# A hybrid decoder step on one core: three halves of the output projection take six mixed tiles first, and the samples' head norm takes one root per partition

## The chip, the cores and the metric

The kernel runs on one core of one Trainium2 chip. The metric is device time in microseconds (us) of one execution, as the median of several runs. Lower is better. Engines are named as in the profile: PE is TensorE's matmul, PEld its weight load, DVE is VectorE, ACT is ScalarE, POOL is GpSimd, and SP is the engine that issues most of the loads.

## The reference

One layer of a decoder, for a prompt of 512 tokens and for 8 samples of one token each (so 520 token columns), with model width 1024:

```python
xn = rmsnorm(x, ln1_w);  z = xn @ w_in                       # q, k, v of group A; q, k, v of group B; out-gate, i, f
attn = moba_attention(qa, k_all, v_all, q_start)             # 8 heads x 64
h, C, n, m = mlstm_chunkwise(qm, km, vm, i_pre, f_pre, ...)  # 4 heads x 128
h = h * lax.rsqrt(jnp.mean(h * h, axis=-1, keepdims=True) + RMS_EPS)
h = h * mlstm_norm_w.reshape(M_HEADS, M_HEAD_DIM)
h = (h.reshape(B, S, MLSTM_WIDTH) * jax.nn.sigmoid(om)).astype(x.dtype)
mix = jnp.concatenate([attn, h], axis=-1)
x = x + mix @ w_out
x = x + jnp.square(jax.nn.relu(rmsnorm(x, ln2_w) @ w_up)) @ w_down
```

A final RMSNorm follows. Outputs are y for prompt and samples, the keys and values of group A, and the new mLSTM states C, n and m. For the samples, the old states C and n are inputs.

## The kernel before

Activations lie transposed: 128 features of one tile on the partitions, the 520 token columns along the free side. Each factor of a product is split in a high and a low fp32r part, and a product is three matmuls (high x high, high x low, low x high), written out in `three` at L869 to L871.

The kernel works through a list of halves, `HALVES`. A half is one tile of 128 output features (`g`) for one part of the tokens: half 0 is the prompt's first 256 tokens, half 1 the other 256 and the 8 samples (264 columns). Entries 0 to 55 are the input projection (g 0 to 27), from 56 on comes the output projection (g 28 to 35). Its first three tiles run half 0 for all three (entries 56, 57, 58) and then half 1 for all three (59, 60, 61), since `LATE_X` is 3. Then both halves of each tile follow. Each half goes over eight tiles k of the inner dimension, 24 matmuls in all, into one of three accumulator banks (`acc`, entry modulo 3), and may start when the half three entries earlier is evacuated (`s_acc_evac`).

For the output projection the inner tiles are the eight mixed tiles: k 0 to 3 are attention (`att_o`), k 4 to 7 the four mLSTM heads. `mixed(k)` makes entry 56 wait for each tile in turn. The heads' tiles are made in tasks `om` and `om_mix`: DVE multiplies by the gate (L2346), ACT rounds to the high part (L1662), DVE subtracts for the low part (L2351). The last two heads are done at slot 55.

`plan()` sets for each entry (slot) the tasks that follow it, and each engine walks the same list in order and does its share of each task. Small results pass through four scratch banks of PSUM (`scr`), used in a ring: `open_job` makes PE wait until the job four places earlier is evacuated, `full` makes a reader wait until the job is written, `free` and `evacuated` report the reading.

The samples' mLSTM output is normalised per head in tasks `sm_den`, `sm_out` and `sm_end`. The values lie as 128 features by 32 columns (8 samples x 4 heads) in `sm_h`. At `sm_out` PE sums the squares over the partitions with a matrix of ones (L1066), with the sum in every partition, and transposes the new n state (L1069). DVE scales the sums and adds eps (L2136), and POOL takes the power -0.5 of all 128x32 values with `rsqrt` (L1814). At `sm_end` DVE waits for POOL (L2142), multiplies (L2143), applies the norm's weights (L2144) and the gate (L2147), and writes the high and low parts into the samples' columns of the mixed tiles (L2151, L2152). The last of these steps raises `s_smp_mix` to 3. PE waits for that ahead of entry 59, the first half 1 of the output projection, and SP ahead of the load of the final norm's weights, which has the last output weights queued behind it.

Weight tiles pass through four slots. ACT makes the high part (L1411) and POOL the low part (L1418) from tile 20 on. Tile 31 is split at slot 56, so in POOL's order its low part stands behind the root of slot 55. SP loads the next weights when `s_w_lo_ok` reaches a count.

From slot 60 on the residual is added and the MLP's input is made: PE transposes the tokens (`xt`, L1214), DVE adds, and tasks `x2` on ACT and DVE scale, split and form the MLP's operands.

Of the kernel before, what the change touches and what calls it, by code (L numbers as in the profile page):

```python
# [24 lines left out]
ALU = mybir.AluOpType  # L25
# [6 lines left out]
P = 128  # L32
# [62 lines left out]
def width(half):  # L95
    return TOK - SPLIT_TOK if half else SPLIT_TOK
# [42 lines left out]
def plan():  # L139
# [3 lines left out]
    def at(s, *names):  # L143
        tasks[s] += names
# [65 lines left out]
        at(51 + two, ("sm_rt", two))  # L210
    at(54, ("sm_den",))
    at(55, ("sm_out",))
    at(56, ("sm_end",))
    for s, j in ((60, 3), (61, 0), (61, 4), (62, 1), (62, 5), (63, 2), (63, 6), (64, 7)):
        if j == 0:
            at(s, ("xt_s",))
# [4 lines left out]
    for t in range(4):  # L221
# [2 lines left out]
    scratch = {  # L224
        "par2": 1, "rstd": 1, "xn": 1, "gates": 1, "gcols": 1, "qs_tok": 1, "qb": 1, "vs_tok": 1, "tokk": 1, "tokv": 1, "tokm": 2,
        "sm_prep": 2, "sm_c": 1, "sm_r": 1, "sm_rt": 1, "ml_m": 1, "ml_k": 3, "ml_o": 2, "ml_t": 1, "ml_mc": 1,
        "sm_den": 1, "sm_out": 2, "ks_tok": 1, "gate": 1, "mx_t": 1, "own": 1, "va_s": 1, "mx_b": 1,
        "zsum": 1, "att_s": 2, "att_t": 3, "att_o": 1, "pv_pick": 1, "pv_end": 1, "xt": 1, "xt_s": 1,
    }
    jobs = {}  # L230
# [132 lines left out]
def build(nc, x_prompt, x_sample, cache_k, cache_v, page_table, state_C, state_n, state_m, ln1_w, w_in,  # L363
# [4 lines left out]
    with ctx:  # L368
# [298 lines left out]
        def free(ins, *key):  # L667
            ins.then_inc(scr_free[JOBS[key] % 4], 1)
# [197 lines left out]
        def _(pe):  # L866
# [34 lines left out]
            def done(mm):  # L901
                mm.then_inc(s_scr_full, 1)
# [15 lines left out]
            def every(col, n=P):  # L918

                return col.to_broadcast([n, P])  # L920
# [30 lines left out]
            def task(name, *a):  # L951
# [111 lines left out]
                elif name == "sm_out":  # L1063
                    pe.wait_ge(s_sm_dve, 2)
                    out = open_job(pe, "sm_out", 0)
                    done(pe.matmul(out[:, 0:NS * MH], every(ones[:, :]), sm_t[:, :, :].rearrange("p a b -> p (a b)"),  # L1066
                                   start=True, stop=True))
                    out = open_job(pe, "sm_out", 1)
                    done(pe.transpose(out[0:NS * MH, 0:P], sm_n[:, :, :].rearrange("p a b -> p (a b)"), ident[:, :]))  # L1069
                elif name == "ml_m":  # L1070
                    h, = a

# [162 lines left out]
            def norm_to_rows():  # L1235

                pe.wait_ge(s_rs2_pow, 2)
                for parts, out in ((range(NT), scr[:, 3, :]), ((NT,), scr[:, 2, :])):
# [3 lines left out]
                                       ident[0:m, 0:m], start=True, stop=True)  # L1242
                    mm.then_inc(s_rows_up, 1)

            def mixed(k):
                if k < 4:
                    evacuated(pe, "att_o", k, 0)
                else:
                    pe.wait_ge(s_mix_lo, k - 3)

            for i in range(N_HALVES):
                if i == 0:
                    pe.wait_ge(s_xs_ok, 1)
                    half_gemm(i, x_parts, x_split_1)
                elif i == WSLOTS:
                    half_gemm(i, x_parts, x_split_0)
                elif i < 2 * N_IN:
                    half_gemm(i, x_parts)
                else:
                    if HALVES[i] == (G_OUT, 1):  # L1260
                        pe.wait_ge(s_smp_mix, 3)
                    half_gemm(i, mix_parts, mixed if i == 2 * N_IN else None)
                for name in TASKS[i]:
                    task(*name)

            def y_to_tok(i, part):

# [543 lines left out]
        def _(pool):  # L1811
            def rsqrt(x, n, free_size):

                return pool.tensor_tensor(x, x, power[0:n, :].to_broadcast([n, free_size]), ALU.pow)  # L1814
# [37 lines left out]
            def task(name, *a):  # L1852
                if name == "score":
                    b, c = a
                    n = 4 * b + c
                    if c == 0:
                        evacuated(pool, "qb", b, 0)
                    for j in (2 * c, 2 * c + 1):
                        pool.wait_ge(kv_in[j], 16 * (b + 1))
                    if n >= 2:  # L1860
                        pool.wait_ge(s_kred_ok, n - 1)
                    pool.tensor_tensor(prod[:, n % 2, :].rearrange("p (j n) -> p j n", j=2),  # L1862
                                       kv[:, 2 * c:2 * c + 2, :],
                                       Qb[:, b % 2:b % 2 + 1, :].to_broadcast([P, 2, AW]), ALU.mult)\
                        .then_inc(s_kmul_ok, 1)
                elif name == "gate":
                    pool.wait_ge(s_kred_ok, 4 * NS)
                    pool.memset(S_wide[:, :, :, :], 0.0).then_inc(s_pv_zero, 1)
                    pool.wait_ge(s_kmul_ok, 4 * NS)
                    pool.memset(vs_split[:, :].bitcast(F32), 0.0).then_inc(s_sel_ok, 1)  # L1870
                elif name == "s_put":
                    b, = a

                    if b >= 4:
                        page_used(pool, b - 4, PAGES - 1)
                    else:
                        pool.wait_ge(s_samp_exp, 1)
                        pool.wait_ge(s_pv_zero, 1)
                    pool.tensor_copy(S_wide[:, b % 4, :, AH * (b % 4):AH * (b % 4 + 1)], S[:, b, :, :])\
                        .then_inc(s_s_put, 1)  # L1880
                elif name == "sm_c":
                    b, = a
                    pool.wait_ge(s_sm_b_ok, 1)
                    pool.wait_ge(C_in[b], 16)
                    pool.tensor_tensor(state(b), state(b), sm_b[:, :, 0, b:b + 1].to_broadcast([P, MH, MD]), ALU.mult)\
                        .then_inc(s_C_decayed, 1)
                elif name == "sm_out":
                    evacuated(pool, "sm_out", 0)
                    rsqrt(sm_t[:, :, :].rearrange("p b h -> p (b h)"), P, NS * MH).then_inc(s_sm_pow, 1)
                elif name == "ml_m":  # L1890
                    h, = a
                    evacuated(pool, "ml_m", h, 0)
                    for j in range(NT):

                        blk = mA[:, A_COL[j]:A_COL[j] + P]
                        pool.affine_select(out=blk, in_=blk, compare_op=ALU.is_ge, fill=0.0, base=0,
                                           pattern=[[1, P]], channel_multiplier=-1).then_inc(s_ml_tri, 1)
                elif name == "ml_n":
                    h, = a
                    pool.wait_ge(s_ml_ms, h + 1)  # L1900
                    rsqrt(m_rs[:, :], P, NT).then_inc(s_ml_pow, 1)
# [54 lines left out]
        def _(dve):  # L1956
            chain = [0]

            def link(ins):

                chain[0] += 1
                ins.then_inc(s_dve_chain, 1)
                dve.wait_ge(s_dve_chain, chain[0])
# [54 lines left out]
            def task(name, *a):  # L2018
# [114 lines left out]
                    dve.tensor_tensor(sm_t[:, :, :], sm_h[:, :, :], sm_h[:, :, :], ALU.mult).then_inc(s_sm_dve, 1)  # L2133
                elif name == "sm_out":
                    out = full(dve, "sm_out", 0)
                    free(dve.tensor_scalar(sm_t[:, :, :].rearrange("p b h -> p (b h)"), out[:, 0:NS * MH],  # L2136
                                           1.0 / MD, EPS, ALU.mult, ALU.add), "sm_out", 0)
                    out = full(dve, "sm_out", 1)
                    free(dve.tensor_copy(n_new_rows[:, :], out[0:NS * MH, 0:P]), "sm_out", 1)
                elif name == "sm_end":  # L2140

                    dve.wait_ge(s_sm_pow, 1)  # L2142
                    link(dve.tensor_tensor(sm_h[:, :, :], sm_h[:, :, :], sm_t[:, :, :], ALU.mult))  # L2143
                    link(dve.tensor_tensor(sm_h[:, :, :], sm_h[:, :, :],  # L2144
                                           par[:, 16:20].unsqueeze(1).to_broadcast([P, NS, MH]), ALU.mult))
                    dve.wait_ge(s_om_sig, MH)
# [522 lines left out]
```

## Time and profile before

| | us |
|---|---|
| median of 3 runs | 751.14 |
| lowest and highest run | 748.95, 752.32 |
| the profiled execution, its own time | 749.44 |
| its span | 747.70 |
| PE busy (share of the span) | 699.8 (94%) |
| PEld busy | 650.9 (87%) |
| DVE busy | 467.4 (63%) |
| ACT busy | 301.6 (40%) |
| POOL busy | 294.8 (39%) |

A time in the trace is in us from the span's start. The span is divided as follows: the input projection, attention, the mLSTM heads and the samples' work up to about 315 us, the output projection from 314.9 to about 375, the MLP up to the end. A row of the trace gives an instruction's start, its duration, engine and line, the operation, and in brackets the idle time of the engine before it and what ended that. Matmuls are pipelined, so the distance between the starts of two is their price, not the duration of one.

### The profile page before, as it was taken

Reading aid. Unit: us, or ns where it says so; the run is one execution under the profiler, and the core shown is the slowest. Engines: PE = TensorE matmul, PEld = TensorE weight load, DVE = VectorE, ACT = ScalarE, POOL = GpSimd, SP = SyncE. Lnnn points to the kernel's source line nnn. Section 1 sums busy time; section 2 is a strip of 40 time slices with the busy share of each in tenths; the row PEclk is TensorE's granted clock in tenths of the full one; section 3 lists DMA queues with packets and bytes.
Section 4 is the critical chain, followed back from the end, with each engine's and each line's share of the span. In section 5 each row is a group of like instructions: output and inputs, shape, how many; then the busy total and the mean of one; then the engine's idle time right before and its main releaser. Section 6 shows DMA issues by size and latency. Waiting matters only on the chain.

```text
span 747.7 us, 15193 instructions
## 1 busy us (share of the span) xinstructions
PE 699.8 (94%) x5537; PEld 650.9 (87%) x5537; DVE 467.4 (63%) x932; ACT 301.6 (40%) x576; POOL 294.8 (39%) x215
## 2 busy tenths in 40 slices
PE   5999789797999999889878999999999999999997
PEld 5988678686878787689868999999999999999996
DVE  4387978766352438434987868575756757586133
ACT  5342454533445223125653544435234433534322
POOL 5225987831232335154002361706144160704531
PEclk8999999998999999989989999999999999999999
DMA  7716998742556968821112232423313141332202
GB/s 243 212 46 208 269 282 249 202 144 74 168 147 197 279 196 176 259 83 61 57 57 60 104 122 59 134 92 113 114 57 112 59 163 59 113 113 85 86 1 115
DMA packets 88634, 100.42 MB, mean 134 GB/s; under 512 B 5374, under 2 KB 64338, under 8 KB 88570
## 3 DMA queue, kind: packets, MB, share of 16 engines
q1 hardware_dynamic: 74566, 92.91, 40.1%
q10 hardware_dynamic: 14004, 6.67, 3.5%
q8 instruction: 39, 0.64, 0.4%
q14 instruction: 25, 0.20, 0.1%
HBM read 92.92 MB, written 6.64 MB: 133 GB/s over the span
## 4 chain that ended last, share of the span: by engine, by line
PE 78%; DVE 11%; ACT 4%; issue 2%; DMA 2%; POOL 1%; SPq 0%; ACTq 0%; DVEq 0%; POOLq 0%
PE acc L869 6%; PE acc L870 6%; PE acc L871 6%; PE acc L1335 5%; PE acc L1334 5%; PE acc L1336 5%; PE acc L1321 4%; PE acc L1320 4%; PE acc L1322 4%; PE scr L1335 3%; PE scr L1334 3%; PE scr L1320 3%; PE scr L1336 3%; PE scr L1322 3%; PE scr L1321 3%
## 5 line engine op out<-in xcount | busy, mean ns | idle before, releaser
L869 PE MATMUL acc<-act_hi,w_hi 128*128 128x256 f32 (+1 forms) x416 | 123.8, 298 | 1.1 <-DVE zT L2411 1.1
L870 PE MATMUL acc<-act_lo,w_hi 128*128 128x256 f32 (+1 forms) x416 | 119.0, 286 | 0.0
L871 PE MATMUL acc<-act_hi,w_lo 128*128 128x256 f32 (+1 forms) x416 | 118.9, 286 | 0.0
L1919 POOL TENSOR_TENSOR h_lo<-relu,h_hi 128x520 fp32r<-128x520 f32 x32 | 43.9, 1373 | 187.6 <-ACT h_hi L1735 187.2
L1862 POOL TENSOR_TENSOR prod<-kv,Qb 128x1024 f32<-128x1024 f32 x32 | 82.8, 2614 | 42.9 <-DVE S L2088 25.2
L869 PEld LDWEIGHTS acc<-act_hi,w_hi 128*128 128x128 f32 x416 | 80.2, 193 | 8.1 <-issue 4.8
L1418 POOL TENSOR_TENSOR w_lo<-raw,w_hi 128x1024 fp32r<-128x1024 f32 x20 | 47.5, 2378 | 96.7 <-ACT w_hi L1411 96.7
L870 PEld LDWEIGHTS acc<-act_lo,w_hi 128*128 128x128 f32 x416 | 80.3, 193 | 0.0
L871 PEld LDWEIGHTS acc<-act_hi,w_lo 128*128 128x128 f32 x416 | 80.0, 192 | 0.0
L2430 DVE TENSOR_TENSOR xT<-acc,xT 128x260 f32<-128x260 f32 x64 | 26.4, 427 | 55.1 <-PE acc L1336 55.1
L2411 DVE TENSOR_TENSOR zT<-acc,rstd 128x264 f32<-128x264 f32 (+1 forms) x56 | 23.5, 423 | 55.6 <-PE acc L871 49.6
L1334 PE MATMUL acc<-h_hi,w_hi 128*128 128x260 f32 x200 | 56.8, 284 | 0.0
L1335 PE MATMUL acc<-h_lo,w_hi 128*128 128x260 f32 x200 | 56.6, 283 | 0.0
L1336 PE MATMUL acc<-h_hi,w_lo 128*128 128x260 f32 x200 | 56.5, 282 | 0.0
L1411 ACT ACTIVATE w_hi<-raw 128x1024 fp32r<-128x1024 f32 x36 | 37.7, 1054 | 37.5 <-PE acc L871 33.4
L1726 ACT ACTIVATE w_hi<-w_sum 128x512 fp32r<-128x512 f32 x47 | 28.7, 627 | 59.6 <-DVE w_sum L2445 25.4
L1734 ACT ACTIVATE relu<-relu 128x520 f32<-128x520 f32 x32 | 20.4, 637 | 70.1 <-DVE relu L2524 70.1
L869 PE MATMUL acc<-mix,w_hi 128*128 128x264 f32 (+1 forms) x128 | 39.0, 305 | 6.2 <-DVE mix L2351 2.9
L2088 DVE TENSOR_REDUCE S<-prod 128x16 f32<-128x1024 f32 x32 | 38.3, 1210 | 8.0 <-POOL prod L1862 8.0
L1335 PE MATMUL scr<-h_lo,w_hi 128*128 128x260 f32 x144 | 40.8, 283 | 0.0
L1334 PE MATMUL scr<-h_hi,w_hi 128*128 128x260 f32 x144 | 40.6, 282 | 0.0
L1336 PE MATMUL scr<-h_hi,w_lo 128*128 128x260 f32 x144 | 40.6, 282 | 0.0
(408 smaller groups left out, 2296.3 us busy)
## 6 DMA issues: line engine op xcount, KB each, us to landing
kv<-in_cache_k_dram SPq DMA_DIRECT2D x64, 256.0 KB, 3.2
kv<-in_cache_v_dram SPq DMA_DIRECT2D x64, 256.0 KB, 3.3
raw<-in_w_up_dram SPq DMA_DIRECT2D x16, 1024.0 KB, 5.5
raw_d<-in_w_down_dram SPq DMA_DIRECT2D x12, 1024.0 KB, 5.0
raw<-in_w_in_dram SPq DMA_DIRECT2D x14, 512.0 KB, 6.0
raw<-in_w_in_dram SPq DMA_DIRECT2D x7, 1024.0 KB, 6.8
x_tok<-in_x_prompt_dram SPq DMA_DIRECT2D x8, 512.0 KB, 9.1
raw<-in_w_out_dram SPq DMA_DIRECT2D x4, 1024.0 KB, 6.4
```

The lines of the kernel that those rows point to most:

```text
L869: pe.matmul(out, w_hi[:, slot, k, :], hi[k][:, cols], start=(n == 0), stop=False)
L870: pe.matmul(out, w_hi[:, slot, k, :], lo[k][:, cols], start=False, stop=False)
L871: mm = pe.matmul(out, w_lo[:, slot, k, :], hi[k][:, cols], start=False, stop=(n == KT - 1))
L1320: pe.matmul(out, u_hi[n % RING][:, k, :], hi[k], start=(k == 0), stop=False)
L1321: pe.matmul(out, u_hi[n % RING][:, k, :], lo[k], start=False, stop=False)
L1322: mm = pe.matmul(out, u_lo[n % RING][:, k, :], hi[k], start=False, stop=(k == 3))
L1334: pe.matmul(out, w[0], h_hi[:, k, cols], start=first, stop=False)
L1335: pe.matmul(out, w[0], h_lo[:, k, cols], start=False, stop=False)
L1336: mm = pe.matmul(out, w[1], h_hi[:, k, cols], start=False, stop=last)
L1418: eng.tensor_tensor(w_lo[:, slot, :, :], raw[:, r_slot, :, side * P:(side + 1) * P], w_hi[:, slot, :, :].bitcast(F32), ALU.subtract).then_ ...
L1862: pool.tensor_tensor(prod[:, n % 2, :].rearrange("p (j n) -> p j n", j=2), kv[:, 2 * c:2 * c + 2, :], Qb[:, b % 2:b % 2 + 1, :].to_broadca ...
L1919: pool.tensor_tensor(h_lo[:, t, :], relu2[:, t % 2, :], h_hi[:, t, :].bitcast(F32), ALU.subtract).then_inc(s_hs_lo, 1)
```

## The change

Three things are edited.

A new function `first_outputs` replaces the loop for entry 56. It runs entries 56, 57 and 58 together: first k 0 to 5 of each of the three, then k 6 and 7 of each. The waits for the mixed tiles stay with entry 56's matmuls. Entries 57 and 58 are skipped in the main loop, and only their tasks are walked.

`sm_out`'s sum of squares exchanges its operands: the squares (128x32) are the weights and one column of ones moves, so 32 sums come out, one on each of 32 partitions. DVE scales them into `mx_col`, and POOL takes the root of 32x1.

A new task `sm_rs` at slot 56 copies the roots to all partitions: PE multiplies the column, broadcast to 128, by a 32x32 identity, into a scratch bank. PE does it between k 6, 7 of entry 57 and k 6, 7 of entry 58, and waits there for POOL. `sm_end`'s first multiplication reads this bank in place of `sm_t`, and a wait on its evacuation stands in place of the chain's step.

```diff
-    at(56, ("sm_end",))
+    at(56, ("sm_rs",), ("sm_end",))
...
                 elif name == "sm_out":
                     pe.wait_ge(s_sm_dve, 2)
                     out = open_job(pe, "sm_out", 0)
-                    done(pe.matmul(out[:, 0:NS * MH], every(ones[:, :]), sm_t[:, :, :].rearrange("p a b -> p (a b)"),
+                    done(pe.matmul(out[0:NS * MH, 0:1], sm_t[:, :, :].rearrange("p a b -> p (a b)"), ones[:, :],
                                    start=True, stop=True))
...
+                elif name == "sm_rs":
+                    pe.wait_ge(s_sm_pow, 1)
+                    out = open_job(pe, "sm_rs", 0)
+                    done(pe.matmul(out[:, 0:NS * MH], every(mx_col[0:NS * MH, :], NS * MH), ident[0:NS * MH, 0:NS * MH],
+                                   start=True, stop=True))
...
+            def first_outputs():
+
+                for ks in (range(6), range(6, KT)):
+                    for i in range(2 * N_IN, 2 * N_IN + LATE_X):
+                        g, half = HALVES[i]
+                        if ks[0] == 0:
+                            pe.wait_ge(s_acc_evac, i - 2)
+                            pe.wait_ge(s_w_lo_ok, g + 1)
+                        for k in ks:
+                            if i == 2 * N_IN:
+                                mixed(k)
+                            three(acc[:, i % 3, 0:width(half)], g % WSLOTS, mix_parts, token_half(half), k, k)
+                        if ks[0] and i == 2 * N_IN + 1:
+                            task("sm_rs")
...
-                else:
+                elif i == 2 * N_IN:
+                    first_outputs()
+                elif i >= 2 * N_IN + LATE_X:
                     if HALVES[i] == (G_OUT, 1):
                         pe.wait_ge(s_smp_mix, 3)
-                    half_gemm(i, mix_parts, mixed if i == 2 * N_IN else None)
+                    half_gemm(i, mix_parts)
                 for name in TASKS[i]:
-                    task(*name)
+                    if name[0] != "sm_rs":
+                        task(*name)
...
                 elif name == "sm_out":
                     evacuated(pool, "sm_out", 0)
-                    rsqrt(sm_t[:, :, :].rearrange("p b h -> p (b h)"), P, NS * MH).then_inc(s_sm_pow, 1)
+                    rsqrt(mx_col[0:NS * MH, :], NS * MH, 1).then_inc(s_sm_pow, 1)
...
                     out = full(dve, "sm_out", 0)
-                    free(dve.tensor_scalar(sm_t[:, :, :].rearrange("p b h -> p (b h)"), out[:, 0:NS * MH],
-                                           1.0 / MD, EPS, ALU.mult, ALU.add), "sm_out", 0)
+                    free(dve.tensor_scalar(mx_col[0:NS * MH, :], out[0:NS * MH, 0:1], 1.0 / MD, EPS, ALU.mult, ALU.add),
+                         "sm_out", 0)
...
                 elif name == "sm_end":
 
-                    dve.wait_ge(s_sm_pow, 1)
-                    link(dve.tensor_tensor(sm_h[:, :, :], sm_h[:, :, :], sm_t[:, :, :], ALU.mult))
+                    out = full(dve, "sm_rs", 0)[:, 0:NS * MH].rearrange("p (b h) -> p b h", b=NS)
+                    free(dve.tensor_tensor(sm_h[:, :, :], out, sm_h[:, :, :], ALU.mult), "sm_rs", 0)
+                    evacuated(dve, "sm_rs", 0)
```

## Rows read from the trace of the kernel before

**Rows 1.** The page's chain that ended last, shares of the span by engine.

```profile
PE 78%; DVE 11%; ACT 4%; issue 2%; DMA 2%; POOL 1%; SPq 0%; ACTq 0%; DVEq 0%; POOLq 0%
```

**Rows 2.** Stretches: length, busy of PE, PEld, DVE, ACT, POOL (count), PEclk, DMA.

```profile
302.10:304.10 2.00, 0.00 (x0) 0.00 (x0) 0.43 (x1) 0.00 (x0) 0.00 (x0) 1.00 0.93 245
...
317.15:319.19 2.04, 0.16 (x2) 0.00 (x1) 1.34 (x3) 1.16 (x2) 0.00 (x0) 1.00 0.00 0
319.19:321.18 1.99, 0.97 (x3) 0.67 (x4) 1.26 (x3) 1.41 (x2) 0.00 (x0) 0.52 0.00 0
321.18:326.04 4.86, 4.86 (x22) 4.86 (x23) 0.78 (x3) 0.17 (x1) 4.61 (x1) 0.50 0.03 7
```

**Rows 3.** Instructions in order of time, PE, 315 to 331: start, duration, line, tiles.

```profile
315.13 0.28 PE L870 MATMUL acc<-mix,w_hi 128*128 128x256 f32 x1
...
317.03 0.28 PE L871 MATMUL acc<-mix,w_lo 128*128 128x256 f32 x1
319.19 0.54 PE L869 MATMUL acc<-mix,w_hi 128*128 128x256 f32 x1 [1.88 <-DVE mix L2351]
...
321.18 0.58 PE L869 MATMUL acc<-mix,w_hi 128*128 128x256 f32 x1 [1.02 <-DVE mix L2351]
...
321.99 0.41 PE L869 MATMUL acc<-mix,w_hi 128*128 128x256 f32 x1
...
325.83 0.41 PE L869 MATMUL acc<-mix,w_hi 128*128 128x256 f32 x1
...
330.25 0.39 PE L869 MATMUL acc<-mix,w_hi 128*128 128x264 f32 x1 [0.57 <-DVE mix L2152]
```

**Rows 4.** Instructions in order of time, DVE, 318 to 323.

```profile
318.44 0.69 DVE L2351 TENSOR_TENSOR mix<-zT,mix 128x512 fp32r<-128x512 f32 x1 [0.70 <-ACT mix L1662]
...
320.43 0.69 DVE L2351 TENSOR_TENSOR mix<-zT,mix 128x512 fp32r<-128x512 f32 x1 [0.70 <-ACT mix L1662]
321.16 0.19 DVE L2136 TENSOR_SCALAR sm_t<-scr 128x32 f32<-128x32 f32 x1
...
322.23 0.42 DVE L2421 COPY xT<-acc 128x256 f32<-128x256 f32 x1 [0.69 <-PE acc L871]
```

**Rows 5.** Instructions in order of time, POOL and DVE, 321 to 330.

```profile
321.43 5.42 POOL L1814 TENSOR_TENSOR sm_t<-sm_t,power 128x32 f32<-128x32 f32 x1 [10.61 <-DVE sm_t L2136]
326.81 2.39 POOL L1418 TENSOR_TENSOR w_lo<-raw,w_hi 128x1024 fp32r<-128x1024 f32 x1
...
326.88 2.36 DVE L2143 TENSOR_TENSOR sm_h<-sm_h,sm_t 128x32 f32<-128x32 f32 x1 [4.23 <-POOL sm_t L1814]
329.28 0.19 DVE L2144 TENSOR_TENSOR sm_h<-sm_h,par 128x32 f32<-128x32 f32 x1
329.50 0.21 DVE L2147 TENSOR_TENSOR sm_h<-sm_h,zT 128x32 f32<-128x32 f32 x1
```

**Rows 6.** Groups by shape, POOL's other roots: count, busy us, mean ns, idle before.

```profile
L1814 POOL TENSOR_TENSOR rs<-rs,power 8x1 f32<-8x1 f32 x2 | 1.4, 717 | 0.0
...
L1814 POOL TENSOR_TENSOR rs<-rs,power 128x4 f32<-128x4 f32 x1 | 1.0, 1006 | 37.6 <-DVE rs L2558 37.6
...
L1814 POOL TENSOR_TENSOR y_ms<-y_ms,power 8x1 f32<-8x1 f32 x1 | 0.5, 542 | 0.0
```

**Rows 7.** Instructions in order of time, POOL and DVE, 308 to 311.

```profile
308.44 2.38 POOL L1418 TENSOR_TENSOR w_lo<-raw,w_hi 128x1024 fp32r<-128x1024 f32 x1 [9.48 <-ACT w_hi L1411]
...
309.98 0.42 DVE L2411 TENSOR_TENSOR zT<-acc,rstd 128x256 f32<-128x256 f32 x1 [2.61 <-PE acc L871]
```

**Rows 8.** One line's instructions, mx_b's copy: ns min/median/max, first and last start.

```profile
L1138 PE MATMUL scr<-ident,mx_col x2: 272/296/319, 183.1 to 183.2; 64*128 64x64 f32 x2
```

**Rows 9.** Instructions in order of time, SP's queue: loads issued after 330.

```profile
330.22 0.34 SPq L825 DMA_DIRECT2D lnf_b<-in_lnf_w_dram  x1
...
339.99 52.88 SPq L846 DMA_DIRECT2D raw<-in_w_up_dram  x4
```

**Rows 10.** The chain that ended last, piece by piece: start, us, what.

```profile
348.02 0.89 PE scr L1214 x8
```

More of the change, by code:

```diff
@@ L226, in plan @@
         "sm_prep": 2, "sm_c": 1, "sm_r": 1, "sm_rt": 1, "ml_m": 1, "ml_k": 3, "ml_o": 2, "ml_t": 1, "ml_mc": 1,
-        "sm_den": 1, "sm_out": 2, "ks_tok": 1, "gate": 1, "mx_t": 1, "own": 1, "va_s": 1, "mx_b": 1,
+        "sm_den": 1, "sm_out": 2, "sm_rs": 1, "ks_tok": 1, "gate": 1, "mx_t": 1, "own": 1, "va_s": 1, "mx_b": 1,
         "zsum": 1, "att_s": 2, "att_t": 3, "att_o": 1, "pv_pick": 1, "pv_end": 1, "xt": 1, "xt_s": 1,
```

## The prediction

> **What bounds the kernel now.** I read the chain that ended last first: TensorE carries 78% of it [rows 1]. So time comes off only where TensorE stands still or runs slowly on that chain. Next I read the granted clock over the start of the output projection, and there TensorE's column shows both faults. From 317.15 to 319.19 us it is busy 0.16 of 2.04 us. From 319.19 to 321.18 it is busy 0.97 of 1.99 us, now at a granted clock of 0.52. From 321.18 to 326.04 it is busy throughout, at 0.50, which is the 1.2 GHz level [rows 2]. TensorE's own instructions give the reasons [rows 3]. At 319.19 and at 321.18 a matmul of half 56 waited for a low part of the mixed tiles (DVE L2351). At 330.25 the first matmul of half 59 waited for DVE L2152, the last step of the samples' head norm. Between two matmuls 0.119 us pass at full clock (16 steps from 315.13 to 317.03), and 0.213 us at half clock (18 steps from 321.99 to 325.83). The stage therefore loses three waits and a slow stretch.
>
> The first two waits follow a VectorE and ScalarE chain. It writes k=6 from 318.44 to 319.13 and k=7 from 320.43 to 321.12 [rows 4]. It doesn't hang on TensorE, and the change leaves it alone. The third wait is that of the head norm. DVE L2136 runs at 321.16 [rows 4]. The root on POOL takes 5.42 us from 321.43. Then POOL starts the low part of weight tile 31 at 326.81 (2.39 us, to 329.20). DVE L2143, a multiplication of 128x32 that starts at 326.88, takes 2.36 us and ends with it at 329.24. The four short operations behind it lead to the matmul at 330.25 [rows 3, 5].
>
> **Part 1, the order of the matmuls.** In place of 18 matmuls (k 0 to 5 of half 56) and a wait, TensorE now has 54 (k 0 to 5 of halves 56, 57, 58) ahead of the first use of k=6. Their weights are there: those of tile 30, the last one needed, were made by POOL from 308.44 for 2.38 us, to 310.82 [rows 7]. The three halves write three accumulators, and the last one that they need free was evacuated before the stage. The number of matmuls and of weight loads doesn't change. The second matmul starts at 315.13, so the 54th starts at 315.13 + 52 x 0.119 = 321.3 and the first of k=6 at 321.4. k=7 is written at 321.12, so neither wait is left, with 0.3 us to spare; if that cover were gone, each tenth would cost a tenth. Half 56 takes its last six matmuls (0.71 us) and ends near 322.2; before, its evacuation started at 322.23 [rows 4], so the DVE isn't served later. Half 57 follows and hands over at 322.8, then the new small matmul, then half 58 to about 323.9.
>
> The slow stretch: 26 matmuls ran between 319.19 and 326.04 at 0.213 in place of 0.119 us, so 26 x 0.094 = 2.4 us. The clock fell right behind a wait of 2.04 us which the change takes away, so I expect the stage at full clock. The price has two bounds: 2.4 us, and nothing, if the clock falls all the same. I take 2.4.
>
> **Part 2, the root on one column.** The sum of squares comes out as 32 partitions of one column, and DVE L2136 and the root work on that. The sum's matmul has the same operands exchanged, with 1 column in place of 32: I take nothing, as it stands among small matmuls of 0.3 us. For the root the nearest rows are 542 ns (8x1, at the end), 717 ns (mean of two 8x1) and 1006 ns (128x4) [rows 6]; 32 columns cost 5.42 us [rows 5], so the price goes with columns. I take 0.54, with 1.01 as the upper bound: POOL ends the root at 321.43 + 0.54 = 321.97, by the bound at 322.44. Both are ahead of 322.8, when TensorE comes to the new matmul, so its wait (with half 58 and all of TensorE queued behind it) costs nothing; the cover is 0.4 to 0.8 us. Nothing else on POOL is behind the root but the low part of tile 31.
>
> **Part 3, the copy to all partitions.** One matmul of fp32, 32 rows deep. The nearest one is mx_b's (64 deep, 64 wide), two passes of 272 to 319 ns of which the second starts 0.1 us behind the first [rows 8]. So about 0.2 us of TensorE's time, with the result at 323.2. It takes one place in the ring of four scratch banks and shifts later jobs by one; all four are evacuated long before and the next job comes at slot 60. Price: nothing.
>
> **Part 4, the samples' end.** The multiplication now reads its factor from PSUM at 323.2 (0.2 us). Its next step, L2144, has two SBUF inputs. POOL now runs the low part of tile 31 from 321.97 to 324.36, across just this. In the trace of before L2143 (two SBUF inputs) stood still until such a POOL operation was over [rows 5], while DVE L2411 at 309.98, with one input in PSUM, took its usual 0.42 us in the midst of one [rows 7]. So L2144 ends at 324.36 + 0.04 = 324.40 and L2147 starts at 324.44. Before, from the start of L2147 to TensorE 0.75 us passed (329.50 to 330.25). Half 59 starts at 325.19. If L2144 weren't held it would be about 324.4; with the root at 1.01 us, 325.66.
>
> The Trainium skill speaks against the change here: its page "SBUF — State Buffer", section "Who interferes with whom", says that a VectorE instruction with two SBUF inputs and a GpSimd one that reads SBUF exclude each other for a whole instruction, and that the one issued first decides. By it an earlier root only moves the collision forward; with it the sum has 325.2, without it 324.4. This trace agrees on L2143 with its 2.36 us.
>
> **The sum.** Half 59 starts at 325.2 in place of 330.25: 5.1 us. The other way round: the stage loses 2.0 + 1.3 us of waits and 2.4 us of slow clock, the last wait grows from 0.7 to 1.3 us (323.9 to 325.2), and 0.2 us of new matmul comes in; 5.7 - 0.6 - 0.2 = 4.9, the same within the rounding of seven terms.
>
> **What it becomes at the end.** From 330.25 on all hangs on TensorE's progress and on smp_mix. The norm weights' load waited for the samples' last step (issued at 330.22, with the last output weights behind it), and the MLP's first loads, held by the low parts of tiles 33 and 35, began at 339.99 [rows 9]. The chain leaves TensorE at the token transposes of 348.02 [rows 10] and then runs through ACT and DVE, each step released by TensorE's halves. I find no transfer with a date of its own there. So 5.1 us are kept. The profiled execution has a span of 747.70 us and a time of 749.44, so 744.3 for it; it is 1.7 below the median of the runs, 751.14, and the prediction goes by the median: 746.0.
>
> **The rivals.** (a) The clock falls all the same. TensorE now waits once for 1.3 us. A wait of 2.0 us at 302.10 left the clock at 1.00, the one at 317.15 was followed by 0.52 [rows 2]. If it falls at 325.2 for as long as before (6.9 us at half speed), 3.4 us are lost: a gain of 1.7, 749.4 us. For it: a single wait did it before. Against it: this one is shorter and stands between busy stretches. If instead only the slow stretch of before was no fixed cost in the runs that set the median, the gain is 5.1 - 2.4 = 2.7, 748.4 us.
> (b) Slower: the root doesn't get cheaper. If a pow on one column took about the 5.42 us, TensorE would stand at the new matmul from 322.8 to 326.9 with half 58 behind it, the low part of tile 31 would hold L2144 to 329.24 and half 59 would start at 330.0, now behind a wait of 4.1 us and at half clock for 6.9 us: 0.2 - 3.4 = -3.2, 754.3 us. It decides once the root takes over 2 us, and becomes a loss near 5. Against it speak all rows of one to four columns [rows 6].
> (c) The change takes hold but the gain is given back at the MLP's start, where the chain is DVE's: a different beat of clock and POOL collisions there. Gain 0 to 2 us, 750 us.
> (d) L2144 isn't held: 0.8 us more, 745.2 us.
>
> **How the numbers follow.** Forecast 0.64, (d) 0.09, (a) 0.15 in both forms, (c) 0.08, (b) 0.04. A measurement can tell about 0.5%, 3.8 us, from no change. The forecast and (d) lie beyond it, and I give them 0.73 together; (a) and (c) lie within, 0.23, of which I move one hundredth to slower for a clock that stays low longer; slower has that and (b), 0.05. The range has the root's bounds and the runs' spread of some 1.7 us on the fast side (743.5), and takes in (a) above, to 749.5.
>
> **What would show it.** After: TensorE busy without a gap from 314.9 to about 323.9 at a granted clock of 1.0; k=6 first used near 321.4; the root near 0.54 us; the new matmul without a wait on POOL; L2144 long (about 1 us) beside the low part of tile 31; half 59 near 325.2; the later stages earlier by the same 5 us, still so at the MLP's start. It is wrong if TensorE waits at the new matmul, if the clock falls behind 323.9, or if the distance between the two traces shrinks between 330 and 400 us.

## The result, and the profile after

The changed kernel takes 745.38 us (median of 6 runs, 744.04 to 746.45) against 750.76 us for the kernel before in the same comparison (6 runs, 747.84 to 752.32). The ratio is 0.9938 with a 95% interval of 0.9915 to 0.9960, so 0.4% to 0.85% faster, about 4.7 us (each ratio below is also to the kernel before, run in the same group). The profiled execution has a time of 745.16 us and a span of 743.4 us. The forecast was 746.0 us in a range of 743.5 to 749.5.

The busy time and the shares of the chain that ended last hardly move: TensorE stays at 78%, as in [rows 1]. An average over the whole kernel doesn't show a change of one stage.

```profile
PE 697.2 (94%) x5539; PEld 647.5 (87%) x5539; DVE 466.0 (63%) x932; ACT 301.5 (41%) x576; POOL 289.8 (39%) x215
PE 78%; DVE 11%; ACT 4%; DMA 3%; issue 2%; POOL 1%; SPq 1%; ACTq 0%; DVEq 0%; POOLq 0%
```

What moved is seen in the stretches of the stage, with the columns of [rows 2] (length, busy PE, PEld, DVE, ACT and POOL with their counts, granted clock, DMA share, GB/s). Half 59 starts at 325.87 here.

```profile
317.15:319.19 2.04, 2.04 (x20) 2.04 (x19) 1.26 (x4) 0.64 (x2) 0.00 (x0) 1.00 0.03 8
319.19:321.18 1.99, 1.99 (x19) 1.99 (x19) 1.30 (x2) 1.16 (x3) 0.00 (x0) 1.00 0.00 0
321.18:324.00 2.82, 2.82 (x25) 2.65 (x23) 1.46 (x4) 0.94 (x1) 1.84 (x2) 1.00 0.02 6
324.00:326.00 2.00, 1.05 (x8) 0.85 (x8) 1.81 (x6) 0.00 (x0) 1.03 (x1) 1.00 0.00 0
```

The waits and the clock of 0.52 and 0.50 of [rows 2] are gone: TensorE is busy throughout up to 324 at full clock, and stands only before 326. Its instructions in order of time (start, duration, line), first and last of each piece (322.10 is the first use of k=6):

```profile
315.61 0.36 PE L869 MATMUL acc<-mix,w_hi 128*128 128x256 f32 x1
...
322.10 0.28 PE L869 MATMUL acc<-mix,w_hi 128*128 128x256 f32 x1
...
323.40 0.28 PE L871 MATMUL acc<-mix,w_lo 128*128 128x256 f32 x1
323.61 0.40 PE L1073 MATMUL scr<-ident,mx_col 32*128 32x32 f32 x2
323.95 0.38 PE L869 MATMUL acc<-mix,w_hi 128*128 128x256 f32 x1
...
324.64 0.28 PE L871 MATMUL acc<-mix,w_lo 128*128 128x256 f32 x1
325.87 0.39 PE L869 MATMUL acc<-mix,w_hi 128*128 128x264 f32 x1 [0.95 <-DVE mix L2176]
```

From the stage's first matmul to half 59 pass 325.87 - 315.61 = 10.26 us; before it was 330.25 - 314.93 = 15.32 us. The stage's first matmul of the kernel before, which stands just ahead of [rows 3]:

```profile
314.93 0.37 PE L869 MATMUL acc<-mix,w_hi 128*128 128x256 f32 x1
```

The same for the norm's path, POOL and DVE, to be held against [rows 4] and [rows 5]:

```profile
321.93 0.15 DVE L2159 TENSOR_SCALAR mx_col<-scr 32x1 f32<-32x1 f32 x1
322.16 0.54 POOL L1837 TENSOR_TENSOR mx_col<-mx_col,power 32x1 f32<-32x1 f32 x1 [10.57 <-DVE mx_col L2159]
322.67 2.36 POOL L1441 TENSOR_TENSOR w_lo<-raw,w_hi 128x1024 fp32r<-128x1024 f32 x1
324.05 0.19 DVE L2166 TENSOR_TENSOR sm_h<-scr,sm_h 128x32 f32<-128x32 f32 x1 [0.62 <-PE scr L1073]
324.28 0.81 DVE L2168 TENSOR_TENSOR sm_h<-sm_h,par 128x32 f32<-128x32 f32 x1
325.12 0.21 DVE L2171 TENSOR_TENSOR sm_h<-sm_h,zT 128x32 f32<-128x32 f32 x1
```

The root takes 0.54 in place of 5.42 us. L2168, the multiplication by the norm's weights, takes 0.81 us, since it ends with POOL's low part of tile 31 (322.67 + 2.36 = 325.03).

**Where the time went, in three sections.** The stage starts at another moment in every execution: ahead of it TensorE waits for loads of the cached values, for 1 to 3 us. In five of the twelve traces (changed, after_third, root16, late_lo, prescaled_again) the granted clock also fell behind this wait, and these five stages start at 314.84 to 316.71, the other seven at 313.23 to 314.93. In the kernel before the clock stayed at 1.00 there [rows 2]; in the changed kernel it did not:

```profile
303.51 2.83 PE L1160 MATMUL acc<-kv,S_wide 128*32 128x512 f32 x4 [2.67 <-DMA kv<-in_cache_v_dram]
```

```profile
304.00:306.00 2.00, 2.00 (x4) 0.18 (x2) 0.00 (x0) 0.00 (x0) 0.00 (x0) 0.50 1.10 361
```

So I cut each trace at two landmarks: the first matmul on the mixed tiles, and POOL's root at the start of the MLP (128x4 and 8x1). In the kernel before and in the changed one:

```profile
392.67 1.87 POOL L1814 TENSOR_TENSOR rs<-rs,power 128x4 f32<-128x4 f32 x2 [37.56 <-DVE rs L2558]
```

```profile
388.37 1.87 POOL L1837 TENSOR_TENSOR rs<-rs,power 128x4 f32<-128x4 f32 x2 [37.56 <-DVE rs L2582]
```

| kernel (one trace each) | start of the stage | to half 59 | start to MLP's root | root to the end |
|---|---|---|---|---|
| before | 314.93 | 15.32 | 77.74 | 355.03 |
| changed | 315.61 | 10.26 | 72.76 | 355.03 |
| changed, again (after_again) | 313.23 | 10.28 | 72.74 | 355.03 |
| changed, third (after_third) | 316.71 | 10.27 | 72.68 | 357.51 |
| order_only | 313.46 | 15.29 | 79.85 | 355.09 |
| root_only | 313.77 | 14.78 | 77.10 | 355.13 |
| wide_root | 313.95 | 15.11 | 79.96 | 355.09 |
| fill_waits | 314.16 | 15.30 | 79.05 | 355.09 |
| root16 | 314.84 | 12.59 | 76.32 | 355.04 |
| late_lo | 315.96 | 9.64 | 72.05 | 355.09 |
| prescaled | 313.27 | 9.17 | 71.60 | 357.43 |
| prescaled_again | 316.46 | 9.18 | 71.62 | 355.12 |

The two middle sections, to half 59 and to the MLP's root, repeat within 0.1 us for the two kernels that were traced more than once, while the start has a spread of 3.5 us. So effects of a few tenths are read from these two sections, and whole times of single executions aren't compared. The other kernels have one trace each. The changed kernel gains 5.06 us up to half 59 and still has 4.98 of it at the MLP's root. That its span is only 4.3 us shorter comes from a start 0.68 us later.

### The profile page after: what moved, and what is told of

It reads as the page before. It is cut to its first block, busy times and chain, and to the rows that moved or that the text cites. A ratio compares the mean times of both kernels' runs of the same rounds, so it can differ in the third digit from the quotient of the medians.

```text
span 743.4 us, 15198 instructions
## 1 busy us (share of the span) xinstructions
PE 697.2 (94%) x5539; PEld 647.5 (87%) x5539; DVE 466.0 (63%) x932; ACT 301.5 (41%) x576; POOL 289.8 (39%) x215
## 4 chain that ended last, share of the span: by engine, by line
PE 78%; DVE 11%; ACT 4%; DMA 3%; issue 2%; POOL 1%; SPq 1%; ACTq 0%; DVEq 0%; POOLq 0%
PE acc L869 6%; PE acc L870 6%; PE acc L871 5%; PE acc L1358 5%; PE acc L1357 5%; PE acc L1359 5%; PE acc L1343 4%; PE acc L1344 4%; PE acc L1345 4%; PE scr L1358 3%; PE scr L1357 3%; PE scr L1343 3%; PE scr L1359 3%; PE scr L1345 3%; PE scr L1344 3%
```

## The experiments

**Each part alone.** My theory was that TensorE's order and the root are two paths that meet at half 59, so that neither part carries the gain. `order_only` has the new function `first_outputs`, without the copy matmul in it, and nothing else. Where it is called:

```diff
+                elif i == 2 * N_IN:
+                    first_outputs()
+                elif i >= 2 * N_IN + LATE_X:
...
-                    half_gemm(i, mix_parts, mixed if i == 2 * N_IN else None)
+                    half_gemm(i, mix_parts)
```

> The new order of the matmuls alone; the root stays at 128x32 (5.42 us on POOL) and no copy matmul is added. Theory (the two parts need each other): the three first halves are done near 323.6 us of the trace of before, but half 59 waits for the samples' norm until 330.0 to 330.3 as before, so the gain is 0 if the clock stays up, and a loss of up to 3.4 us if TensorE's wait of 6.6 us lets the clock fall for 6.9 us: 750 to 754 us against 750.8. Rival (the order alone carries the gain, by taking away 3.3 us of waits and 2.4 us of slow clock): about 746 us.

Measured: 751.37 us, ratio 1.0016 (0.9997 to 1.0035). TensorE finishes its three halves early and then stands 6.5 us for the norm, and behind that wait it runs at half clock. First its instructions, then the stretches:

```profile
321.96 0.28 PE L871 MATMUL acc<-mix,w_lo 128*128 128x256 f32 x1
328.75 0.59 PE L869 MATMUL acc<-mix,w_hi 128*128 128x264 f32 x1 [6.51 <-DVE mix L2167]
...
333.32 0.42 PE L871 MATMUL acc<-mix,w_lo 128*128 128x264 f32 x1
333.54 0.32 PE L869 MATMUL acc<-mix,w_hi 128*128 128x264 f32 x1
```

```profile
328.70:333.50 4.80, 4.75 (x21) 4.75 (x22) 0.66 (x2) 0.00 (x0) 0.00 (x0) 0.50 0.63 220
333.50:336.00 2.50, 2.50 (x22) 2.50 (x21) 0.43 (x1) 1.06 (x1) 0.67 (x1) 0.98 0.59 207
```

Half 59 is not a tenth earlier than before (15.29 against 15.32 us), and the 21 matmuls at 0.22 in place of 0.12 us cost 2.1 us, which is the 79.85 against 77.74 of the table. So the new order alone brings nothing up to half 59, and loses 2.1 us behind it in this trace; the runs' interval reaches from no loss to 2.6 us. The rival of 746 us falls: it lies outside the interval.

`root_only` is the other half: the narrow root and the copy matmul, with the old order of the halves. Against the changed kernel:

```diff
-            def first_outputs():
...
-                elif i == 2 * N_IN:
-                    first_outputs()
-                elif i >= 2 * N_IN + LATE_X:
+                else:
...
+                    half_gemm(i, mix_parts, mixed if i == 2 * N_IN else None)
                 for name in TASKS[i]:
-                    if name[0] != "sm_rs":
-                        task(*name)
+                    task(*name)
```

> The root on 32 partitions of one column and the copy matmul alone; the halves stay in their order, the copy follows half 56. Theory: the waits for k=6 and k=7 and the slow clock stay, three halves end near 329.7 as before, the samples' norm is long done, so only the wait of 0.7 us ahead of half 59 goes and 0.2 to 0.4 us of matmul comes in: 0.3 to 0.5 us gained, 750.4 us, the same within the noise. Rival (the root carries the gain): 746 to 747 us.

Measured: 750.11 us, ratio 0.9993 (0.9974 to 1.0012); 14.78 us to half 59, and 77.10 to the MLP's root, 0.64 us less than before. TensorE's two waits are there as before, and so is the half clock, in this trace for 3.4 us:

```profile
318.10 0.38 PE L869 MATMUL acc<-mix,w_hi 128*128 128x256 f32 x1 [1.96 <-DVE mix L2357]
320.10 0.39 PE L869 MATMUL acc<-mix,w_hi 128*128 128x256 f32 x1 [1.37 <-DVE mix L2357]
```

```profile
321.20:324.60 3.40, 3.40 (x17) 3.38 (x17) 2.49 (x5) 0.00 (x0) 1.97 (x1) 0.50 0.04 10
324.60:328.50 3.90, 3.90 (x34) 3.90 (x34) 0.42 (x1) 0.00 (x0) 0.00 (x0) 1.00 0.76 248
```

The norm is written at 323.96, long before half 59 at 328.55, and TensorE's own path is what ends last. I had expected 0.3 to 0.5 us, and part of the agreement is luck: the copy matmul cost TensorE about 0.7 us here (with a wait of 0.17 for POOL), not 0.2 to 0.4, while the slow stretch held 16 matmuls in place of 26. Read at the MLP's root, in one trace each, the parts alone bring -2.1 and +0.6 us, together +5.0.

**Is the slow stretch a consequence of the two waits?** `fill_waits` is the kernel before, with matmuls in the waits whose output nobody reads:

```diff
             def mixed(k):
+                for n in range({6: 15, 7: 9}.get(k, 0)):
+                    pe.matmul(acc[:, 3, 0:256], w_hi[:, 0, 0, :], mix_parts[0][0][:, 0:256], start=True, stop=True)
```

> The kernel before, with 15 matmuls of 128x256 that nobody reads ahead of k=6 of half 56 and 9 ahead of k=7, so that TensorE works through most of the two waits (1.8 of 2.0 us and 1.1 of 1.3 us). Theory (the slow stretch is the consequence of these waits): the granted clock stays at 1.0 from 319 to 326 us, 26 matmuls take 0.119 in place of 0.213 us, half 59 starts up to 2.4 us earlier, bounded by the samples' norm, which ends as before at 330.2: so the trace shows the three halves done near 327 and the wait ahead of half 59 grown from 0.7 to 3.1 us, and the time stays at 750.8 within 0.5 us. Rival (the clock falls for another reason): the clock is 0.5 there all the same. Second rival (the clock falls one stretch later, behind the longer wait ahead of half 59): up to 3 us slower.

Measured: 751.82 us, ratio 1.0025 (1.0008 to 1.0042).

```profile
316.38 1.95 PE L1247 MATMUL acc<-mix,w_hi 128*128 128x256 f32 x15
318.88 1.23 PE L1247 MATMUL acc<-mix,w_hi 128*128 128x256 f32 x9
320.43 0.38 PE L869 MATMUL acc<-mix,w_hi 128*128 128x256 f32 x1 [0.32 <-DVE mix L2353]
329.46 0.59 PE L869 MATMUL acc<-mix,w_hi 128*128 128x264 f32 x1 [2.72 <-DVE mix L2154]
```

```profile
319.19:326.04 6.85, 6.54 (x55) 6.33 (x55) 1.50 (x4) 1.40 (x2) 5.37 (x1) 1.00 0.01 2
...
329.40:332.20 2.80, 2.73 (x12) 2.74 (x13) 0.67 (x3) 0.00 (x0) 0.00 (x0) 0.50 0.51 154
```

(The first fence is TensorE in order of time, the second the stretches.) With the waits filled, the clock is 1.00 from 319 to 326, where it was 0.50 before [rows 2]. So the waits brought it down, and the first rival falls. But half 59 starts no earlier (15.30 us): what TensorE gained there it now waits for the norm, 2.72 in place of 0.57 us. That gain is 2.2 us and not 2.4, because the first three of the 26 slow matmuls, those of k=6, only shortened the wait for k=7. And this wait brings the clock down behind half 59, for 12 matmuls, which costs 1.3 us (79.05 against 77.74). My time of 750.8 plus or minus 0.5 missed the measured 751.82 for that reason, and the second rival, that the clock falls one stretch later, was right.

**The root's price, and the wait for it.** `wide_root` and `root16` are the changed kernel with 32 and 16 columns in the root; only column 0 is used. The edit for 32 (the copy matmul then reads the same column of `sm_t`):

```diff
...
-                    free(dve.tensor_scalar(mx_col[0:NS * MH, :], out[0:NS * MH, 0:1], 1.0 / MD, EPS, ALU.mult, ALU.add),
+                    free(dve.tensor_scalar(sm_t[0:NS * MH, 0, 0:1], out[0:NS * MH, 0:1], 1.0 / MD, EPS, ALU.mult, ALU.add),
...
-                    rsqrt(mx_col[0:NS * MH, :], NS * MH, 1).then_inc(s_sm_pow, 1)
+                    rsqrt(sm_t[0:NS * MH, :, :].rearrange("p b h -> p (b h)"), NS * MH, NS * MH).then_inc(s_sm_pow, 1)
```

> The changed kernel, but POOL takes the root of 32 columns on 32 partitions (31 of the columns are not used). If the price goes with columns the root takes about 5.4 us, TensorE stands about 4 us at the copy matmul with half 58 behind it, and half 59 starts 4.8 us later than in the changed kernel: 750 us if the clock stays up, up to 753.6 if it falls for 6.9 us. If the price goes with partitions or with all elements, 1.4 us (a quarter of 5.4): 0.5 us slower than the changed kernel at most, 745.5 to 746 us.

> The changed kernel with a root of 16 columns on 32 partitions (15 of the columns are not used). At 0.157 us a column on top of 0.38 us the root takes 2.9 us, TensorE stands 1.6 us at the copy matmul and then 1.3 us ahead of half 59, which starts 2.3 us later than in the changed kernel. If these two waits leave the clock up: 747.7 us. If they bring it down to half for some 3 us or more: 749 us or later.

Measured: wide_root 751.04 us, ratio 1.0016 (0.9999 to 1.0034); root16 748.42 us, ratio 0.9989 (0.9977 to 1.0000). The roots, wide_root first, then root16:

```profile
320.50 5.41 POOL L1837 TENSOR_TENSOR sm_t<-sm_t,power 32x32 f32<-32x32 f32 x1 [10.58 <-DVE sm_t L2159]
```

```profile
321.39 2.89 POOL L1837 TENSOR_TENSOR sm_t<-sm_t,power 32x16 f32<-32x16 f32 x1 [10.59 <-DVE sm_t L2159]
```

128x32 took 5.42 us [rows 5], 32x32 takes 5.41, 32x16 2.89 and 32x1 0.54: 0.157 us for each column beyond the first, and at 32 columns the same for 32 as for 128 partitions. The price goes with columns; the other reading (1.4 us for a quarter of the elements) falls. TensorE in root16, its instructions and then the stretch behind half 59's start:

```profile
324.32 0.40 PE L1073 MATMUL scr<-ident,sm_t 32*128 32x32 f32 x2 [1.42 <-POOL sm_t L1837]
...
327.43 0.59 PE L869 MATMUL acc<-mix,w_hi 128*128 128x264 f32 x1 [1.79 <-DVE mix L2176]
```

```profile
327.40:330.20 2.80, 2.77 (x12) 2.78 (x13) 0.64 (x2) 0.00 (x0) 0.00 (x0) 0.50 0.52 163
```

Half 59 is 2.3 us later than in the changed kernel, as expected, and 12 matmuls at half clock make 3.6 us of it at the MLP's root (76.32 against 72.7). The measured 748.42 us lies between my two times, 747.7 and 749, since the clock fell for 2.8 us. The second wait was 1.8 us where I had 1.3: the copy holds TensorE back by 1.5 us only, half 59 comes 2.3 us later, and the difference is added to the 0.95 us that TensorE waits there anyway. Why half 59 moves by the whole length of the root is seen on the norm's path, in POOL and DVE of root16:

```profile
324.25 2.35 POOL L1441 TENSOR_TENSOR w_lo<-raw,w_hi 128x1024 fp32r<-128x1024 f32 x1
```

```profile
324.99 1.65 DVE L2168 TENSOR_TENSOR sm_h<-sm_h,par 128x32 f32<-128x32 f32 x1
```

The low part of tile 31 starts when the root ends, and L2168 ends when the low part ends. By this chain half 59 moves with the root one for one, from the first tenth, and both runs bear it out: a root 2.35 us longer moves it by 2.33 us in root16, and one 4.87 us longer by 4.85 in wide_root. In wide_root TensorE waits 3.95 us at the copy, the clock is down from half 58 to 334.3, and the MLP's root is 7.2 us later than in the changed kernel, 2.2 us later than before:

```profile
325.96 0.63 PE L1073 MATMUL scr<-ident,sm_t 32*128 32x32 f32 x2 [3.95 <-POOL sm_t L1837]
```

So the price of an expensive root is its own length plus a slow stretch, and in the new order the slow stretch turns it into a loss in this trace. The runs' interval for wide_root reaches from no loss to 2.6 us.

**The hold by POOL's low part, and a faster version.** `late_lo` makes POOL wait with the low part of tile 31 until the samples' columns are written. `prescaled` also does the two multiplications by the norm's weights and by the gate at `sm_out`, ahead of the root's result, while DVE waits.

```diff
+                    if n == 31:
+                        pool.wait_ge(s_smp_mix, 3)
                     weight_lo(pool, n, n % WSLOTS, n // 2 % 2)
```

```diff
                     free(dve.tensor_copy(n_new_rows[:, :], out[0:NS * MH, 0:P]), "sm_out", 1)
+                    link(dve.tensor_tensor(sm_h[:, :, :], sm_h[:, :, :],
+                                           par[:, 16:20].unsqueeze(1).to_broadcast([P, NS, MH]), ALU.mult))
+                    dve.wait_ge(s_om_sig, MH)
+                    link(dve.tensor_tensor(sm_h[:, :, :], sm_h[:, :, :], by_sample(zT[:, OM:OM + MH, SEQ:TOK]),
+                                           ALU.mult))
...
                     evacuated(dve, "sm_rs", 0)
-                    link(dve.tensor_tensor(sm_h[:, :, :], sm_h[:, :, :],
-                                           par[:, 16:20].unsqueeze(1).to_broadcast([P, NS, MH]), ALU.mult))
-                    dve.wait_ge(s_om_sig, MH)
-                    link(dve.tensor_tensor(sm_h[:, :, :], sm_h[:, :, :], by_sample(zT[:, OM:OM + MH, SEQ:TOK]),
-                                           ALU.mult))
```

> The changed kernel once more, as the yardstick for the other three of this group. 745.4 us, half 59 10.2 to 10.3 us behind the first matmul on the mixed tiles, VectorE's multiplication by the norm's weights held for 0.8 us by the low part of tile 31.

> The changed kernel with POOL's low part of weight tile 31 held back until the samples' columns are written. Theory (the low part holds the multiplication by the norm's weights for its whole length): the multiplication takes 0.2 in place of 0.81 us and half 59 starts 0.6 us earlier, 9.65 us behind the first matmul on the mixed tiles; the time falls by 0.6 us, 744.8 us, which the trace can show and the median hardly. The low part ends 2.5 us later than before, and the load queued behind it still lands before its use. Rival (the multiplication is long for another reason, such as its operand broadcast): it stays at 0.8 us and nothing moves. Rival of the late load: the low part, now late, delays a later weight tile and the time rises.

> As the version with the late low part, and the two multiplications by the norm's weights and by the gate are done before the root, while VectorE waits, so three steps are left behind the copy matmul. Theory: half 59 starts another 0.45 us earlier, 9.2 us behind the first matmul on the mixed tiles, and TensorE's last wait shrinks from 1.2 to 0.2 us: 744.3 us, the fastest of all. Rival: the added steps delay the evacuation of half 56 and nothing is gained; or the half-us is taken back at the start of the MLP.

Measured in one group: after_again 744.58 us, ratio 0.9931 (0.9916 to 0.9946); late_lo 744.94, 0.9935 (0.9921 to 0.9950); prescaled 744.67, 0.9932 (0.9920 to 0.9945). The hold is shown by late_lo's DVE and POOL:

```profile
324.40 0.19 DVE L2168 TENSOR_TENSOR sm_h<-scr,sm_h 128x32 f32<-128x32 f32 x1 [0.62 <-PE scr L1073]
324.62 0.19 DVE L2170 TENSOR_TENSOR sm_h<-sm_h,par 128x32 f32<-128x32 f32 x1
...
325.62 2.40 POOL L1441 TENSOR_TENSOR w_lo<-raw,w_hi 128x1024 fp32r<-128x1024 f32 x1 [2.58 <-DVE mix L2178]
```

The same multiplication (L2170 here) takes 0.19 in place of 0.81 us once POOL is idle, so the operand's broadcast isn't its price. Half 59 comes after 9.64 us, and in prescaled after 9.17 us, each as expected. The medians don't show it: I had expected 744.3 us for prescaled as the fastest of all, and it took 744.67 beside 744.58 for the changed kernel. Its trace has an odd section behind the MLP's root: 357.43 in place of 355.03 us, in a stretch of slow clock. Whether the earlier stage caused that was the open question of the last group.

> The prescaled version again. Its stage took 9.17 us, but behind the root at the start of the MLP its trace had a stretch at a granted clock of 0.59 and lost 2.4 us there, and its median stood level with the changed kernel's. Theory (that stretch is a matter of the single execution): the profile has the MLP's rest at 355.1 us from that root to the end, like all other kernels here, and the median comes out 0.5 to 1.1 us below that of the changed kernel, within the noise. Rival (the earlier stage brings the MLP's start into a beat in which the clock falls): the stretch is there again, 357.4 us from the root to the end, and the medians are level again.

> The changed kernel beside it, as the yardstick: 744.5 to 745.4 us, 10.3 us from the first matmul on the mixed tiles to half 59, and 355.0 us from the root at the MLP's start to the end.

Measured: prescaled_again 743.99 us, ratio 0.9897 (0.9869 to 0.9925); after_third 747.65 us (four of its seven runs at 747.65 to 748.60, the other three at 742.32 to 745.93), ratio 0.9925 (0.9896 to 0.9955). For after_third both the time, 744.5 to 745.4 us, and the 355.0 us behind the root were missed: the slow stretch had changed sides. The 7.5 us that begin 2.5 us behind the MLP's root, first in prescaled_again, then in after_third:

```profile
390.58:398.08 7.50, 6.18 (x50) 5.83 (x49) 4.62 (x8) 2.19 (x4) 1.33 (x1) 1.00 0.28 98
```

```profile
391.89:399.39 7.50, 6.18 (x33) 5.74 (x32) 2.72 (x6) 1.79 (x3) 0.89 (x1) 0.59 0.28 98
```

The same kernel has it in one execution and not in another, so it doesn't belong to prescaled. It costs 2.4 us when it comes. What decides whether it comes was not tried. The traces give a hint: TensorE waits for the MLP's root for 1.06 to 1.86 us, and the slow stretch followed two of the three longest of these waits, 1.86 in prescaled and 1.79 in after_third. It didn't follow the 1.79 of root16, nor the shorter ones. By the stage's own length prescaled is 1.1 us faster than the changed kernel in both of its traces. Its median stood level once and 3.7 us lower once, where I had expected 0.5 to 1.1 and the changed kernel's median lay high; I take the 1.1 us from the traces, and the two intervals of its ratio don't contradict it.

## Why the prediction was right

**The sum.** I had half 59 at 325.19 with the stage starting at 314.93, so 10.26 us; three traces have 10.26, 10.28 and 10.27. The steps on the way, counted from the stage's first matmul, forecast and measured:

| step | forecast | measured |
|---|---|---|
| first use of k=6 | 6.5 | 6.49 |
| POOL's root ends | 7.04 | 7.09 |
| TensorE comes to the copy matmul | 7.9 | 8.00 |
| DVE reads the copied roots | 8.3 | 8.44 |
| L2144, now L2168, ends | 9.47 | 9.48 |
| half 59 | 10.26 | 10.26 |

The root took its lower price, 0.54 us. That the copy came 0.1 us late, and took about 0.5 us of TensorE's time (the two steps from 323.40 to 324.17, at full clock 0.24) where I had 0.2, cost nothing: L2168 had to wait for POOL anyway. The cover of k=7 was larger than my 0.3 us, which I had counted to the first use of k=6; k=7 is used at 322.45 and was written at 321.90, so 0.55 us.

**The waits for k=6 and k=7** vanished, and the clock stayed at 1.00. fill_waits shows that the slow stretch came from these waits, which I had only read from the order of the two. How long it lasts isn't fixed: 26 matmuls in the trace of before, 16 in that of root_only.

**A step that was right in its result and loose in its reason.** I checked the sum the other way round, as waits of 3.3 us plus 2.4 us of slow clock minus the new costs. With the last wait among its terms this is a complete account of TensorE's time. But the experiments show that the terms aren't gains one by one: filling the waits gave back the slow stretch, 2.2 us, and moved half 59 by nothing, and taking away the first two waits and the slow stretch by order alone moved it by nothing either, since the last wait grew to 6.5 us. In the kernel before two paths end within 0.6 us of each other, TensorE's at 329.7 and the norm's at 330.2. Only the step that follows both paths to half 59 carries the forecast.

**Rivals.** (a), the clock falls behind the last wait: not in any of the three traces of the changed kernel, with waits of 0.95 to 0.97 us; it did behind the waits of 1.4 and 1.8 us of root16, the 2.7 of fill_waits and the 6.5 of order_only. My row for it, the wait at 302.10 that left the clock at 1.00, was one execution: behind the same wait for loads the clock fell in two of the three traces of the changed kernel. (b), an expensive root: the mechanism is real, as wide_root shows, with a loss of 2.2 us in the trace where I had 3.2. My two thresholds were both too high. The gain turns into a loss near 3.9 us and not near 5, an estimate on a straight line between root16 (2.9 us, still 1.4 us of gain, 76.32 against 77.74) and wide_root (5.4 us, 2.2 us of loss). And it begins to shrink with the first tenth, not at 2 us: the cover of 0.9 us at the copy matmul (322.70 to 323.61) protects TensorE, but not the norm's path, where the low part of tile 31 and L2168 follow the root. Part 4 had this, with 325.66 for a root of 1.01 us; rival (b) didn't use it. (c), the gain is given back at the MLP: 0.08 us of it is; but a slow stretch of 2.4 us stands there in one of the three traces of the changed kernel (357.51 against 355.03). (d), L2144 isn't held: it is, for as long as POOL's operation lasts, and late_lo frees it.

**The whole.** 4.7 us by the ratio against 5.1; the interval of the ratio, 3.0 to 6.4 us, holds both, and the two medians differ by 5.4. So the mechanism is confirmed by the sections of the traces, to 0.1 us; the runs' times can only say that the size fits.

## What to carry to other kernels

Where two paths end close together at one instruction, follow each to that instruction and take the later one; waits on one path that are added up promise a gain that the other path takes. A part tried alone then says "no use" twice, while both together are worth 5 us. When a wait on TensorE is removed or moved, ask what the next wait will be and how long: a longer one can cost a slow stretch behind it on top of itself. Here that cost 1.3 us behind a wait of 2.7 us, and 2.1 us behind one of 6.5.

## What the runs showed of the hardware that I had not expected

A power on POOL costs 0.157 us a column beyond the first and nothing for partitions, from 32x1 (0.54 us) over 32x16 (2.89) to 32x32 (5.41) and 128x32 (5.42). Some roots take longer than this line, and why was not tried: of the kernel before's five roots of 128x4, four took 1.0 us and one 1.9. So where many partitions need the same value, a root in one column and a copy by TensorE can pay: the copy matmul took 0.40 us.

Within one kernel the stage's length repeats to 0.1 us, but its start differs by up to 3.5 us between executions, and at the MLP's start a stretch at a granted clock of 0.59 costs 2.4 us in some of them. Both add to the scatter of the times. That neither comes from the change is not shown: each was seen in single executions of the changed kernel and its variants, and the kernel before has only one trace.

The same length of wait doesn't always have the same effect on the clock. I looked at the last wait before each fall in the twelve traces, at three places: the loads ahead of the stage, the stage, and the MLP's root. Behind every wait of 2.58 us or more it was down, behind waits of 1.79 to 2.39 us in some executions and not in others. Behind shorter ones it fell once, in root_only, where 1.37 us followed a wait of 1.96 us that had left it up.
